# SSD stage: the six projection tiles of a group in the order x, x, B, C, z, z, one and a half of them in each chunk

## What is computed

```python
z, xbc = first columns of (u @ w_in_2)            # 2048 columns z, 2048 + 1024 + 1024 columns x, B, C
xbc = silu(causal_dwconv(xbc, conv_w, conv_b))    # width 4, along the tokens
# 8 groups; a group has 4 heads of 64 (256 columns of x and of z), 128 columns of B and 128 of C
# chunks of 128 tokens
CB      = C @ B.T                                  # per chunk and group
y_diag  = (CB * L) @ (x * dt)                      # L = exp of differences of cumulated decays, lower triangle
state   = state * decay + B.T @ (decay * x * dt)   # carried from chunk to chunk
y       = y_diag + C @ state * exp(a_cs) + D_skip * x
y       = rmsnorm(y * silu(z))                     # norm per group of 256 columns
```

## Time and profile before

| | us |
|---|---|
| median of 3 runs | 2858.71 (2848.5 to 2859.33) |
| the profiled execution | 2839.74 |
| its span, first to last instruction | 2837.9 |
| PE busy in the span | 2519.9 (89%) |
| DVE busy in the span | 1214.8 (43%) |
| SSD groups 0 to 7, first transpose to the first gate product | 1148.91 to 1599.50 |

### The profile page before, as it was taken

One profiled execution on the slowest core, in us unless ns is written; L12 is line 12 of the kernel. 1 busy time (PEld: TensorE's weight loads), 2 busy tenths in 40 slices (PEclk: granted clock), 3 DMA queues, 4 the chain that ended last, 5 costly groups with the idle time before them and its releaser, 6 DMA issues.

```text
span 2837.9 us, 26766 instructions
## 1 busy us (share of the span) xinstructions
PE 2519.9 (89%) x9522; PEld 1641.5 (58%) x9522; DVE 1214.8 (43%) x2013; ACT 719.3 (25%) x1121; POOL 721.8 (25%) x515
## 2 busy tenths in 40 slices
PE   5999996899989779788887799986799999999995
PEld 3885344688868556666666673574344444445443
DVE  4545333399960454666767430125611221122113
ACT  3334343333331233323333230222111111111111
POOL 2330003133433223322222121130322222222221
PEclk8997678899999899989999799997999999999998
DMA  3222000155542123212121103112189999999994
GB/s 122 74 76 103 0 1 30 59 178 178 178 149 88 37 76 89 60 45 60 45 60 60 30 30 142 66 34 82 57 314 331 340 349 346 319 338 352 337 304 147
DMA packets 169821, 403.51 MB, mean 142 GB/s; under 512 B 12224, under 2 KB 99264, under 8 KB 145792
## 3 DMA queue, kind: packets, MB, share of 16 engines
q1 hardware_dynamic: 149136, 342.27, 33.9%
q0 software_dynamic: 19440, 55.79, 8.1%
q10 hardware_dynamic: 1152, 4.19, 0.4%
HBM read 378.62 MB, written 39.32 MB: 147 GB/s over the span
## 4 chain that ended last, share of the span: by engine, by line
PE 77%; DVE 11%; DMA 6%; ACT 2%; issue 2%; POOL 1%; POOLq 0%; SPq 0%; DVEq 0%; ACTq 0%
PE bank L704 33%; PE bank L695 26%; PE bank L862 3%; DMA arena<-u_rows,rows_in 3%; PE bank L802 2%; PE bank L779 2%; PE bank L1112 2%; DVE hn L1648 2%; PE bank L721 2%; DVE arena L1890 1%; PE bank L956 1%; DMA arena<-in_w_up 1%; PE bank L793 1%; DVE arena L1779 1%; PE bank L783 1%
## 5 line engine op out<-in xcount | busy, mean ns | idle before, releaser
L695 PE MATMUL bank<-arena 128*128 128x512 f32 x1840 | 813.4, 599 | 9.2 <-DMA arena<-in_w_br_ssd 6.4
L695 PEld LDWEIGHTS bank<-arena 128*128 128x128 f32 x1840 | 348.5, 192 | 422.4 <-issue 418.1
L607 POOL TENSOR_TENSOR w_low_flat<-arena,in_high 128x1024 fp32r<-128x1024 f32 (+1 forms) x73 | 183.5, 2536 | 489.0 <-ACT in_high L1400 489.0
L704 PE MATMUL bank<-in_x,in_high 128*128 128x512 f32 (+1 forms) x584 | 243.5, 417 | 18.3 <-DVE x_low L1841 15.2
L2118 DVE TENSOR_TENSOR arena<-arena,bank 128x256 f32<-128x256 f32 x62 | 26.1, 421 | 490.8 <-ACT arena L1608 490.8
L704 PE MATMUL bank<-in_x,w_low_flat 128*128 128x512 f32 (+1 forms) x584 | 235.3, 403 | 0.0
L704 PE MATMUL bank<-x_low,in_high 128*128 128x512 f32 (+1 forms) x584 | 235.3, 403 | 0.0
L654 POOL DMA_INDIRECT y_rows<-arena,rows_out x62 | 98.9, 1595 | 493.0 <-DVE arena L2130 232.0
L704 PE MATMUL bank<-x_high,w_high 128*128 128x512 f32 x352 | 141.1, 401 | 14.1 <-DVE x_low L1655 13.0
L591 POOL TENSOR_TENSOR w_low<-arena,w_high 128x2048 fp32r<-128x2048 f32 x22 | 103.0, 4684 | 175.0 <-ACT w_high L1319 175.0
L704 PEld LDWEIGHTS bank<-in_x,in_high 128*128 128x128 f32 (+1 forms) x584 | 113.1, 194 | 51.7 <-issue 21.3
(11 more groups left out here) (316 smaller groups left out, 4391.6 us busy)
## 6 DMA issues: line engine op xcount, KB each, us to landing
arena<-in_we_gate SPq DMA_DIRECT2D x62, 1024.0 KB, 5.8
arena<-in_we_up SPq DMA_DIRECT2D x62, 1024.0 KB, 7.8
arena<-in_we_down SPq DMA_DIRECT2D x62, 1024.0 KB, 8.6
arena<-in_w_in SPq DMA_DIRECT2D x40, 1024.0 KB, 5.4
arena<-in_w_ada SPq DMA_DIRECT2D x12, 2048.0 KB, 8.2
arena<-in_w_up SPq DMA_DIRECT2D x22, 1024.0 KB, 11.4
arena<-in_w_in SPq DMA_DIRECT2D x18, 512.0 KB, 4.9
arena<-in_w_out SPq DMA_DIRECT2D x4, 2048.0 KB, 7.9
```

Of the source, the lines that this page charges most:

```text
L607: pool_eng.tensor_tensor(in2_tile(j, "low"), in2_tile(j, "whole"), in2_tile(j, "high").bitcast(f32), ALU.subtract).then_inc(S("w_low"), 1)
L695: ins = nc.tensor.matmul(out, w(k), rhs(k), start=first and k == 0, stop=last and k == nk - 1)
L704: ins = nc.tensor.matmul(out, w, x, start=k == 0 and n == 0, stop=k == KD - 1 and n == 2)
```

## The change

The tiles of a group now come in the order x, x, B, C, z, z, for weights, banks, semaphore counts and readers alike. A chunk multiplies one and a half tiles (`PARTS`): chunk 0 the first x and slices 0 to 3 of the second, chunk 1 its slices 4 to 7 and B, chunk 2 C and slices 0 to 3 of the first z, chunk 3 its slices 4 to 7 and the second z. The readers take the tiles that a chunk completes (`FILL`): one, two, one, two. The silu of C is now called behind the tile of chunk 2; in the six tiles ahead of the loop it comes in front of the first z.

```diff
@@ panels
         for g in range(SG):
-            add_half_panel(one(w_in2, 0, KD, 256 * g, 256 * g + 256), PRODUCTS["ssd"] + 6 * g + 2)
-            add_half_panel(one(w_in2, 0, KD, 2048 + 256 * g, 2048 + 256 * g + 256), PRODUCTS["ssd"] + 6 * g + 4)
+            add_half_panel(one(w_in2, 0, KD, 2048 + 256 * g, 2048 + 256 * g + 256), PRODUCTS["ssd"] + 6 * g + 2)
             add_half_panel([(w_in2, 0, KD, 4096 + P * g, 4096 + P * g + P, 256, 0),
-                            (w_in2, 0, KD, 5120 + P * g, 5120 + P * g + P, 256, P)], PRODUCTS["ssd"] + 6 * g + 6)
+                            (w_in2, 0, KD, 5120 + P * g, 5120 + P * g + P, 256, P)], PRODUCTS["ssd"] + 6 * g + 4)
+            add_half_panel(one(w_in2, 0, KD, 256 * g, 256 * g + 256), PRODUCTS["ssd"] + 6 * g + 6)
@@ s_freed, tables
-            return (S("z_read"), 2 * g + j + 1) if j < 2 else (S("s_taps"), 3 * (4 * g + j - 1))
+            return (S("z_read"), 2 * g + j - 3) if j >= 4 else (S("s_taps"), 3 * (4 * g + j + 1))
-        FILL = ((0, 1), (2,), (3, 4), (5,))
+        FILL = ((0,), (1, 2), (3,), (4, 5))
+        PARTS = (((0, 0, 8), (1, 0, 4)), ((1, 4, 8), (2, 0, 8)), ((3, 0, 8), (4, 0, 4)), ((4, 4, 8), (5, 0, 8)))
@@ tensor
+            def project_part(i, k0, k1):
+                if k0 == 0:
+                    pe.wait_ge(*s_freed(i - 2))
+                    pe.wait_ge(S("w_low"), W_LOW["in2"] + SSD_TILE + i + 1)
+                high, low = in2_tile(SSD_TILE + i, "high"), in2_tile(SSD_TILE + i, "low")
+                for k in range(k0, k1):
+                    for n, (w, x) in enumerate(((high, in2_x[k][:, :]), (high, x_low[:, k, :]), (low, in2_x[k][:, :]))):
+                        ins = nc.tensor.matmul(banks[i % 2][:, :], w[:, k, :], x, start=k == 0 and n == 0,
+                                               stop=k == KD - 1 and n == 2)
+                if k1 == KD:
+                    ins.then_inc(S("product"), 1)
...
-                        for i in FILL[c]:
-                            project(6 * (g + 1) + i)
+                        for i, k0, k1 in PARTS[c]:
+                            project_part(6 * (g + 1) + i, k0, k1)
@@ scalar and vector, read_tile and the chunk loop
+                if j == 4 and waiting:
+                    xbc_silu()
...
-            xbc_silu()
             for g in range(SG):
...
-                        if c == TT - 1:
+                        if c == 2:
                             xbc_silu()
```

More of the change, by code:

```diff
@@ L1450, in xbc_silu @@
                 i, buf = waiting.pop(0)
-                q = 4 * (i // 6) + i % 6 - 2
+                q = 4 * (i // 6) + i % 6
                 act.wait_ge(*s_freed(i))
@@ L1462, in read_tile @@
                     act.wait_ge(S("y_gated"), 2 * (g - 1))
-                if j < 2:
-                    nc.scalar.activation(ssd["zs"][:, 2 * s + j, :], banks[i % 2][:, :], ACT.Tanh,
+                if j >= 4:
+                    nc.scalar.activation(ssd["zs"][:, 2 * s + j - 4, :], banks[i % 2][:, :], ACT.Tanh,
                                          scale=0.5).then_inc(S("z_tanh"), 1)
-                    if j == 1:
+                    if j == 5:
                         in2_high_part(SSD_UNIT + i // 2 + 2)
                     return
-                ch = {2: 2 * g, 3: 2 * g + 1, 4: 16 + g, 5: 24 + g}[j]
-                buf = {2: ssd["xs"][:, 2 * s, :], 3: ssd["xs"][:, 2 * s + 1, :], 4: ssd["B"][:, s, :],
-                       5: ssd["C"][:, s, :]}[j]
+                ch = {0: 2 * g, 1: 2 * g + 1, 2: 16 + g, 3: 24 + g}[j]
+                buf = {0: ssd["xs"][:, 2 * s, :], 1: ssd["xs"][:, 2 * s + 1, :], 2: ssd["B"][:, s, :],
+                       3: ssd["C"][:, s, :]}[j]
                 nc.scalar.activation(buf, banks[i % 2][:, :], ACT.Identity, scale=col("conv_w2", 3 * 32 + ch),
                                      bias=col("conv_b2", ch)).then_inc(S("s_tap3"), 1)
-                if j in (3, 5):
+                if j in (1, 3):
                     in2_high_part(SSD_UNIT + i // 2 + 2)
@@ L1897, in read_tile @@
                 s = g % 2
-                if j < 2:
-                    zs = ssd["zs"][:, 2 * s + j, :]
-                    dve.wait_ge(S("z_tanh"), 2 * g + j + 1)
+                if j == 4 and waiting:
+                    xbc_silu()
+                if j >= 4:
+                    zs = ssd["zs"][:, 2 * s + j - 4, :]
+                    dve.wait_ge(S("z_tanh"), 2 * g + j - 3)
                     nc.vector.scalar_tensor_tensor(zs, zs, 1.0, banks[i % 2][:, :], ALU.add, ALU.mult)\
@@ L1903, in read_tile @@
                     return
[L1904 to L1907, removed]
+                ch = {0: 2 * g, 1: 2 * g + 1, 2: 16 + g, 3: 24 + g}[j]
+                buf = {0: ssd["xs"][:, 2 * s, :], 1: ssd["xs"][:, 2 * s + 1, :], 2: ssd["B"][:, s, :],
+                       3: ssd["C"][:, s, :]}[j]
+                dve.wait_ge(S("s_tap3"), 4 * g + j + 1)
                 for back in (1, 2, 3):
@@ L1915, in read_tile @@
                     xbc_silu()
-                waiting.append((4 * g + j - 2, buf))
+                waiting.append((4 * g + j, buf))
             def heads(ap, width):
```

## The result

The changed kernel took 2755.8 us (median of 4 runs, 2747.16 to 2770.78) against 2858.16 us for the kernel before (4 runs), a ratio of 0.9655 with a 95% interval of 0.9606 to 0.9703: faster by 3.4%. The profiled execution took 2747.16 us with a span of 2745.3, 92.6 us under the span before.

The account below looks back on a forecast made before the run. PE, busy 89% of the span, bounds the kernel, losing time to waits and low clock. Gain: group 0's 8.4 plus seven groups' 86.8 less group 7's 3.8, 91 us; median 2858.7 - 91.4 = 2767 us, range 2748 to 2793.

Parts of the forecast that it names:

- Group 0's wait and clock: Start of group 0: the wait of 8.38 us goes, covered by the two z tiles; 8.4 us gained.
- The group without its waits, 46.6: A group with tiles, summed over its chunks at the high clock without waits, takes 46.6 us instead of 59.1.
- The long wait: PE's wait for the silu of C ahead of every group, 7.32 us, 8.38 at group 0, was to go.
- The 1.8 us wait: PE's wait for M in chunk 1, 1.80 us per group, to be replaced by 0.1 us at chunk 0.
- M of chunk 3 has 2.2 us to spare: M of chunk 3 ready by T + 45.2, PE asking at T + 47.4; T is the second z product's end.
- The chain laid out from T: Times of DVE, POOL and PE work in a group, counted from T, the end of the second z tile's product.
- The split costs nothing: Two split tiles per group cost nothing, the number of blocks being equal; bound above 2.4 us over seven groups.
- Group 7 gives 3.8 us back: Group 7, without tiles: M of chunk 0 comes 10.4 us into the group, before 6.56; 3.8 us lost.
- The clock comes back: Groups with tiles: the low clock behind the long wait, 3.4 us per group, goes; PEclk in a group is 1.00.
- by that, short waits cost no clock: Rule on PE's clock: behind waits of 1.80 us matmuls kept short times, so short waits cost no clock.
- The second: Rival: chunk 0 still waits, M coming 2 to 2.5 us later; gain 71 us, 2788 us; chance 0.15.
- The fourth: Rival: the long wait only moves, M of chunk 3 being late; gain 16 us, 2842 us; chance 0.04.

Follow-up runs that it names:

- experiment 5: Changed kernel with the second x tile split after six slices instead of four; ratio 0.9672 to the kernel before, groups 46.49 us apart.
- experiment 3: Changed kernel with the silu of C called in the loop behind chunk 3's two z tiles, no longer behind chunk 2; ratio 0.9854 to the kernel before.
- experiment 2: Kernel before, old tile order and silu of C last, but with one and a half tiles per chunk; ratio 0.9948 to the kernel before.
- experiment 4: Changed kernel with the second x tile split after two slices instead of four; one run, 2764.08 us.
- experiment 6: Changed kernel with ACT's rounded high part made later, so POOL's low parts do not run beside the two gatings; one run, 2752.06 us.
- experiment 1: Changed kernel's tile order and early silu of C, but whole tiles, 2, 1, 2, 1 per chunk; ratio 0.9832 to the kernel before.

## Why the prediction was right, point by point

- **The result.** 2767 was forecast with 2748 to 2793; 2755.8 was measured, in runs from 2747 to 2771. The gain was forecast as 91.4 us; the medians lie 102.4 apart, and the interval of the ratio spans gains of 85 to 113. The trace is the closer test: the first gate product came 91.34 us earlier, and the span shrank by 92.6. That the first of these agrees to 0.1 us is partly luck, since errors cancel. Of the 91.34 us, 0.6 lie ahead of the stage, which began earlier. Group 0's wait and clock gave 8.5 (8.4 forecast), the seven groups 7 x 12.18 = 85.2 (86.8), and group 7 took back 3.0 (3.8).
- **The group without its waits, 46.6.** 46.92 with a wait of 0.34, 46.49 without one (experiment 5). The sum from rows of one group held. The seven groups gave 1.6 us less than forecast because of the wait, 0.34 and not 0.1.
- **The long wait goes** because the silu of C leaves the group's end: shown by experiment 3 (with the silu late again a wait of 4.38 us comes back) and by experiment 2 (in the old order with the old place it is 7.32 as before).
- **The 1.8 us wait is replaced by that of chunk 0.** Right. Forecast 0.1, measured 0.34: the gatings ended 8.3 us after the last z product, not 8.0. The estimate took POOL's pair at its length beside short instructions; beside the longer gatings it took 5.20 and not 4.93. Experiments 4 and 5 move the wait by the cover, experiment 6 by POOL.
- **M of chunk 3 has 2.2 us to spare.** It was ready at 1277.40, and PE asked for it at 1279.37: 2.0 us. DVE, then PE:

```profile
1276.71 0.69 DVE L1975 TENSOR_TENSOR arena<-arena 128x512 f32<-128x512 f32 x1
```

```profile
1279.37 0.45 PE L986 MATMUL bank<-arena 128*64 128x128 f32 x4
```

  The chain laid out from T held: M of chunk 2 was there at T + 31.4 and the silus of B and C ended at T + 40.8, both as forecast, and M of chunk 3 was there at T + 45.0 (45.2 forecast). Only the next T was misplaced, at 47.4, where the prediction's own group is 46.7 us long; by that the reserve would have been 1.5 us.
- **The split costs nothing.** Experiment 5 shows it, beside the group with whole tiles of experiment 1.
- **Group 7 gives 3.8 us back.** M of its chunk 0 came 10.6 us into the group instead of 6.56, 4.1 us later where 3.8 were forecast. Group 7 became only 3.0 us longer (39.9 against 36.9). The other 1.0 us lies behind that M, where the way to the gates took 29.3 us and not 30.4, and it is the clock. The decay matmuls of chunk 3, before and of the change:

```profile
1590.46 2.07 PE L956 MATMUL bank<-arena,shp 32*128 32x128 f32 x8
```

```profile
1500.05 1.15 PE L971 MATMUL bank<-arena,shp 32*128 32x128 f32 x8
```

  With the same waits behind the first M, this stretch took 29.0 to 30.3 us in experiments 1 to 6. So this 1.0 us can't be put down to the change; it was luck.
- **The clock comes back**, 3.4 us per group: PEclk is 1.00 over each of groups 0 to 6, and PE was busy there for 3.4 us less. The sentence that the prediction took from the Trainium skill's page "TensorE: Matmul & The Clock Gate", section "A second HAM failure mode: psum-queue depth-cycling", that small idle gaps suffice to make the clock swing, did not come true at gaps of 0.34 us; experiments 1 and 4 show it for gaps of 2.72 and, once, 1.74 us.
- **The step that was too simple** is the one on the rows of 1.80: "by that, short waits cost no clock". It held for the 14 waits in the two main traces, seven of 1.80 us and seven of 0.25 to 0.35, and the forecast needed it only for the small wait at chunk 0. But in experiment 4 one of seven waits of 1.64 to 1.74 us cost 3.2 us of clock, and in experiment 1 waits of 2.72 us cost 0.1 to 4.8. Had the new wait been 1.7 us, the forecast could have been off by this.
- **The rivals.** None took place. The second, that chunk 0 waits 2.5 us, was nearest: experiment 4 shows that two slices less of cover would have made most of it. The fourth counted DVE's work in a group as 38.5 us from a window of 58 us; a whole group has 40.4, before and after. Within 46.9 us that still left no wait at chunk 3.

## What to carry to other kernels

Where one engine is to stay busy, put the product whose readers have the longest chain first and the one with the shortest last, and spread the cover so that each wait has about as much behind it as its chain is long; a matmul accumulation can be cut to get there; cuts after two, four and six of eight slices showed no cost of their own here. Work out when each answer is ready from the end of the last product, with the slow durations beside GpSimd where they overlap, and compare it with when it is asked for: the sum for one group was good to 0.3 us. The last turn of such a loop has no next group to take cover from; give it the first tiles of what follows.

## What was not expected of the hardware

- The cost of a fallen clock varies much between equal waits: behind 2.72 us it was 0.1 us once and 1.7 to 4.8 six times, behind 4.38 it was 3.7 to 3.8, behind 7.32 3.5 (before) to 3.9 (experiment 2) on average, behind 1.74 nothing five times and 3.2 once. What decides it, no experiment here shows. An average over groups, such as the 3.4 us of the prediction, hides this.
- GpSimd and VectorE slow each other both ways: GpSimd's pair of instructions took 4.73 us beside three taps, which read a bank, and 5.20 beside the two gatings, so the delay of VectorE is longer than one computes from GpSimd's free length.
